# A two-layer generator backbone on one core: layer-1 modulation products taken out of layer 0, the others placed between token projections, half of the first output projection placed around the layer norm

## The reference, cut to what matters

```python
for i in range(DEPTH):                      # two layers
    mod_l = (c_act @ mod_w[i] + mod_b[i]).reshape(b, N_MOD, 1, d)
    mod_c = (c_ctx_act @ mod_w[i] + mod_b[i]).reshape(N_MOD, d)
    hl = modulate(rms_norm(xl, norm_g[i, 0]), mod_l[:, 0], mod_l[:, 1])
    if i % 2 == 0:
        yl = even_mixer(hl, *ew); yc = even_mixer(hc, *ew)
    else:
        ...                                 # latent attention and differential attention
    xl = xl + mod_l[:, 2] * yl
    h2l = modulate(rms_norm(xl, norm_g[i, 1]), mod_l[:, 3], mod_l[:, 4])
    xl = xl + mod_l[:, 5] * moe(h2l, ...)

def even_mixer(h, ...):
    u = h @ w_in                            # 1024 -> 1536
    y_conv = conformer_conv(u[..., :1024], ...)   # value * sigmoid(gate), 31 taps, layer norm, silu
    y_pool = pool_mix(u[..., 1024:], ...)         # windows 2, 4, 8, 16, then a 128 x 128 product per group
    return concatenate([y_conv, y_pool], -1) @ w_out
```

## Time and profile before

| | us |
|---|---|
| median of 3 runs | 1004.16 |
| lowest, highest | 1004.1, 1006.32 |
| the profiled execution | 1001.35 |
| its span | 999.6 |
| PE busy in the span | 861.9 (86%) |
| DVE, ACT, POOL busy | 322.8, 175.0, 184.0 |
| DMA traffic | 298.00 MB, mean 298 GB/s |

### The profile page before, as it was taken

The page is one execution under the profiler, slowest core; times in us unless marked ns, Lnnn a source line. Parts: engine busy times, 40 slices in busy tenths (PEclk is TensorE's granted clock), DMA queues, the critical chain, the costliest instruction groups (busy, mean ns, idle before and its releaser), DMA issues.

```text
span 999.6 us, 10053 instructions
## 1 busy us (share of the span) xinstructions
PE 861.9 (86%) x3779; PEld 384.6 (38%) x3779; DVE 322.8 (32%) x699; ACT 175.0 (18%) x465; POOL 184.0 (18%) x212
## 2 busy tenths in 40 slices
PE   1799989997999999887849999796696999978776
PEld 0444435444733333222228443354545433322222
DVE  1269996213511221110123331636305111111010
ACT  2400033212200000000032111535503000000000
POOL 3100690122112123201121220301111111111000
PEclk9899998998899999897969999999797899989998
DMA  9981289954799999999989105270247799999993
GB/s 366 408 324 71 84 365 424 429 212 168 264 359 403 338 397 406 392 405 419 422 347 372 54 24 229 91 330 1 81 172 251 275 404 408 412 420 426 414 421 135
DMA packets 33111, 298.00 MB, mean 298 GB/s; under 512 B 6464, under 2 KB 6770, under 8 KB 16156
## 3 DMA queue, kind: packets, MB, share of 16 engines
q1 hardware_dynamic: 26064, 283.26, 70.1%
q0 software_dynamic: 6912, 13.92, 4.0%
q10 hardware_dynamic: 76, 0.02, 0.0%
HBM read 293.66 MB, written 12.58 MB: 306 GB/s over the span
## 4 chain that ended last, share of the span: by engine, by line
PE 67%; DMA 18%; DVE 4%; ACT 3%; issue 3%; SPq 2%; POOL 1%; DVEq 0%; ACTq 0%; POOLq 0%
PE bank L1099 17%; PE bank L460 9%; DMA ring<-in_gu_pack 9%; PE bank L1001 8%; PE bank L1122 7%; PE bank L1192 6%; DMA ring<-in_mod_pack 6%; PE bank L938 5%; DMA B<-in_gu_pack 4%; PE bank L1203 3%; SPq L890 2%; PE bank L1050 2%; PE bank L965 2%; PE bank L948 1%; PE bank L540 1%
## 5 line engine op out<-in xcount | busy, mean ns | idle before, releaser
L1099 PE MATMUL bank<-ring,hT 128*64 128x512 f32 x704 | 208.1, 624 | 27.0 <-issue 18.2
L1803 DVE SCALAR_TENSOR_TENSOR hT<-hT,WORK,bank 128x256 f32<-128x256 f32 x34 | 16.3, 480 | 324.9 <-ACT hT L1360 312.2
L1099 PEld LDWEIGHTS bank<-ring,hT 128*64 128x64 f32 x704 | 61.8, 143 | 128.3 <-issue 126.4
L1887 DVE SCALAR_TENSOR_TENSOR WORK<-WORK,par 128x512 f32<-128x512 f32 x116 | 90.7, 860 | 0.0
L460 PE MATMUL bank<-ring,hT 128*128 128x512 f32 (+2 forms) x256 | 88.0, 499 | 0.7 <-ACT hT L1333 0.7
L1001 PE MATMUL bank<-ring,B 128*128 128x512 f32 x192 | 83.3, 594 | 0.0
L1122 PE MATMUL bank<-ring,WORK 128*64 128x512 f32 x352 | 79.9, 595 | 1.0 <-ACT WORK L1365 1.0
L1365 ACT ACTIVATE WORK<-bank 128x256 f32<-128x256 f32 x34 | 13.1, 384 | 279.3 <-PE bank L1108 279.3
L938 PE MATMUL bank<-ring,cs 128*32 128x512 f32 x384 | 48.7, 653 | 14.6 <-DMA ring<-in_mod_pack 14.6
L1192 PE MATMUL bank<-hT,ring 128*128 128x512 f32 x128 | 57.4, 612 | 2.9 <-ACT hT L1414 2.9
L460 PEld LDWEIGHTS bank<-ring,hT 128*128 128x128 f32 x256 | 46.0, 190 | 35.9 <-issue 34.0
(11 more groups left out here) (270 smaller groups left out, 1041.0 us busy)
## 6 DMA issues: line engine op xcount, KB each, us to landing
ring<-in_gu_pack SPq DMA_DIRECT2D x42, 2048.0 KB, 21.5
ring<-in_mod_pack SPq DMA_DIRECT2D x24, 2048.0 KB, 18.7
ring<-in_down_pack SPq DMA_DIRECT2D x21, 2048.0 KB, 29.6
WORK<-in_gu_pack SPq DMA_DIRECT2D x6, 2048.0 KB, 28.8
ring<-in_wout_pack SPq DMA_DIRECT2D x4, 2048.0 KB, 18.7
ring<-in_win_pack SPq DMA_DIRECT2D x3, 2048.0 KB, 36.8
X<-in_gu_pack SPq DMA_DIRECT2D x3, 2048.0 KB
B<-in_gu_pack SPq DMA_DIRECT2D x3, 2048.0 KB
```

What stands on the lines that cost most here:

```text
L1099: mm = pe.matmul(dst[ST * x:ST * x + ST, :], HG[L][s][:, k, :], columns(units[x], 512 * k, 512), start=k == 0, stop=k == KC - 1)
L1887: ins = dve.scalar_tensor_tensor(out=acc, in0=src, scalar=w, in1=acc, op0=ALU.mult, op1=ALU.add)
```

## The change

Only two pairs of layer-1 weights are moved to stand behind the first MoE (with the one that stood there already), and two more behind the layer-1 projection weights. Mods 2 to 5 are placed between the groups of value, gate and pool products, each turn one group behind its product. The products with the pooled half of the output projection's depth are made ahead of the convolution's transposes (tiles 0 and 1) and behind them (tile 2). One layer-1 mod (6) stays in layer 0, 7 stands behind the MoE, 8 and 9 among the projections, 10 and 11 in eight parts in the differential attention. The columns of mods 0, 1, 6 to 11 are written by DVE in one instruction. The order of the squares in layer 1 is split around the copy of mod 7.

```diff
@@ stream_plan
-    out += pair(1, 0) + [("wout", 0, 0)] + pair(1, 1) + [("wout", 0, 1)] + pair(1, 2)
+    out += [("wout", 0, 0)] + pair(1, 0) + [("wout", 0, 1)]
     out += expert_units(0)
-    out += pair(1, 3)
+    out += pair(1, 1)
     for kind in OIN:
         out.append(("oin", kind))
     out.append(("lora",))
-    out += pair(1, 4) + pair(1, 5)
+    for v in (2, 3, 4, 5):
+        out += pair(1, v)
@@ generator_kernel, banks
+        MOD_BANK = (6, 6, 6, 6, 6, 6, 7, 6, 6, 6, 7, 7)
-        OUT_BANKS = ((4, 5), (0, 1))
+        OUT_BANKS = ((4, 5, 6), (0, 1))
@@ project_pe
                 if i == MOD_ITEM:
-                    mod_multiply(10)
+                    mod_multiply(8)
+                elif i == MOD_ITEM + 4:
+                    mod_turn(8)
                 elif i == len(ITEMS):
-                    mod_multiply(11)
+                    mod_multiply(9)
@@ attention_pe
                     turn_o(i - 3)
+                if i == 2:
+                    mod_turn(9)
+                if 8 <= i < 16:
+                    mod_in_attention(i - 8)
                 if 0 <= i - 1 < n_units:
                     probs(i - 1)
@@ attention_scalar
+                if i == 12:
+                    mod_copy(10)
...
+            mod_copy(11)
@@ tensor: new functions
+            def mod_in_attention(j):
+
+                i, part = 10 + j // 4, j % 4
+                if part == 0:
+                    for h in (0, 1):
+                        loaded(pe, where[("mod",) + MOD_PAIRS[i] + (h,)])
+                    pe.wait_ge(sem("mod_cols"), 10)
+                    pe.wait_ge(sem("mod_rows"), i)
+                mm = mod_part(i, MOD_BANK[i], (2 * part, 2 * part + 1))
+                if part == 3:
+                    mm.then_inc(sem("mod_mm"), 1)
@@ tensor: layer 0
-            for i in range(2, 6):
-                mod(i)
+            for m in (0, 1):
+                value_gate(m, 1)
+                value_gate(m, 0)
+            mod_multiply(2)
+            value_gate(2, 1)
+            mod_turn(2)
+            mod_multiply(3)
+            value_gate(2, 0)
+            mod_turn(3)
+            value_gate(3, 1)
+            value_gate(3, 0)
+            pool_rows(0)
+            mod_multiply(4)
+            pool_rows(1)
+            pool_rows(2)
+            mod_turn(4)
+            pool_rows(3)
+            mod_multiply(5)
+            mod_turn(5)
 
             pe.wait_ge(sem("pool_w_in"), 16)
+            pe.wait_ge(sem("pool_in"), 4)
             pe.wait_ge(sem("pooled"), 4)
...
-            mod(6)
+            def out_half(i, ks):
+
+                h, j = divmod(i, NT)
+                w = slot(where[("wout", 0, h)])
+                loaded(pe, where[("wout", 0, h)])
+                for k in ks:
+                    mm = pe.matmul(bank[OUT_BANKS[0][i % 3]][:, :], mixT[:, (k + 4) % KC, j * P:(j + 1) * P], w[:, (k + 4) % KC, :], start=k == 0, stop=k == KC - 1)
+                return mm
+            pe.wait_ge(sem("mod_cols"), 6)
+            gates("a0", 0, 2, (0, 1), (6, 7))
+            pe.wait_ge(sem("pool_out"), 4)
+            out_half(0, range(4))
+            out_half(1, range(4))
             pe.wait_ge(sem("conv_done"), 4)
...
+            out_half(2, range(4))
+            mod_multiply(6)
+            pe.wait_ge(sem("ln_rows"), 4)
...
+            mod_turn(6)
+            for i in range(8):
+                if i >= 3:
+                    pe.wait_ge(sem("out_used"), i - 2)
+                    out_half(i, range(4))
+                for k in range(4, KC):
+                    if i == 0:
+                        pe.wait_ge(sem("mix_done"), k - 3)
+                    mm = out_half(i, (k,))
+                mm.then_inc(sem("out_mm"), 1)
...
-            mod(9)
+            mod(7)
@@ scalar: layer 1
-            mod_rows(9)
-            square_rows("a1")
+            square_rows("a1", (0, 1))
+            mod_copy(7)
+            square_rows("a1", (2, 3))
@@ vector: columns in one instruction, norm_rows
+            def mod_columns(i):
+
+                L, v = MOD_PAIRS[i]
+                r = R_MODB + 48 * L + 8 * v
+                dve.wait_ge(sem("mod_turned"), i + 1)
+                tt(mods[:, L, v, :, :].rearrange("p (h c) s -> p h c s", h=2), bank[7][:, 0:16].rearrange("p (c h s) -> p h c s", c=4, h=2),
...
                 if tag == "a1":
-                    for j in range(4):
+                    for j in (0, 1):
+                        scaled(tag, j)
+                    mod_columns(7)
+                    norm_scale(1, 0)
+                    for j in (2, 3):
                         scaled(tag, j)
```

More of the change, by code:

```diff
@@ L173, in slot_plan @@
             free = [at for at in free if at not in LENT]
+        if n > RING and all(stream[held[at]] in early or stream[held[at]][0] == "wout" for at in free if at in held) and len(free) == RING:
+            free.sort(key=lambda at: early.index(stream[held[at]]) if stream[held[at]] in early else len(early) + held[at])
         at = free.pop(0)
@@ L989, in moe_gates, with project_out @@
                     mm.then_inc(sem("gate_mms"), 1)
-            def project_out(L, lhs, tiles, first=0, between=None):
+            def project_out(L, lhs, tiles):
                 for h in range(2):
@@ L1178, in _, with value_gate @@
             mod(1)
-            for m in range(4):
+            def value_gate(m, part):
                 n = where[("win", m // 2)]
```

161 lines of the change are left out of this document (79 added, 82 removed).

## The result

| | before | after |
|---|---|---|
| median (4 runs each) | 1004.13 | 991.35 |
| lowest, highest | 1001.14, 1006.32 | 988.34, 994.82 |
| the profiled execution | 1001.35 | 988.34 |
| its span | 999.6 | 986.5 |

The ratio is 0.9888, 95% interval 0.9857 to 0.9919: the change gains 12.8 us of the median. The forecast, 1006, was wrong, and so was its sign; the time lies 0.15 us outside the range. Rival A, with 993.5, describes it.

A forecast was written before the change was run, and what follows sets the result against it. The way to the first expert product and the stretch between the MoEs bound the kernel. Terms +3.1 - 3.8 + 2.4 = +1.7 on the profiled 1001.35 gave 1003.0; the median's 2.8 above made it 1006, range 991.5 to 1009.5.

The forecast's parts named there:

- Rival A: Layer 0: POOL is served at once, `pooled` stays at 149.95; -10.7 in all, 993.5, chance 0.35.
- What bounds the kernel: The MoE moves as a block; the way to the first expert product and the stretch between the MoEs count.
- Step 1: Start of layer 0: eight small column operations become one on DVE, whose first block comes 0.8 us earlier.
- Step 2: Layer 0: POOL's third group starts 75.0 behind DVE's first block, after POOL was idle 1.0 us.
- Step 3a: Layer 0: POOL is shut out through DVE's last run; `pooled` at 162.4 instead of 149.95, layer 0's end +3.1.
- Step 4: Layer 0, from the pool products to the end of the output projection: 74.9 us.
- Step 5: Behind the first MoE: two squares ahead of mod 7's copy and columns on DVE bring -3.8 us.
- Step 6: Layer 1's projections and attention: turns and copies of the moved mods cost +2.4 us, quarters hidden.

The follow-up runs named there:

- e11_before_yield: The kernel before, with one break in DVE's run at tap 10 of the third block; 1003.66, ratio 1.0014.
- e1: The changed kernel, with POOL waiting for DVE's count of taps ahead of its groups three and four; 1002.78, ratio 0.999.
- e4: The changed kernel with no half of the output projection ahead of the layer norm; 992.15, ratio 0.9889.
- e6: The changed kernel with layer 1's squares not split, mod 7's copy ahead of all four; 995.09, ratio 0.9919.
- e7: The changed kernel with every quarter of mods 10 and 11 made twice, the second time with zeros; 995.08, ratio 0.9929.
- e9: The changed kernel with mod 7's columns on ACT again and the squares not split; 994.36, ratio 0.9914.
- e8: The kernel of e3 with one break in DVE's run, at tap 10 of the third block; 984.78, ratio 0.9831.
- e12: Mods 2 to 5 behind the pooled groups, DVE's break at tap 5, slots given out in the change's order; 992.03, ratio 0.9909.
- e10: The changed kernel in its own order, with one break in DVE's run at tap 23 of the third block; 987.83, ratio 0.9887.
- e5: The kernel of e2, with POOL's requests placed by waits on DVE's count of taps; one run, 1002.06.
- e2: The changed kernel with the first pooled groups ahead of the last block's value and gate products on PE; 991.64, ratio 0.9875.
- e3: The changed kernel with mods 2 to 5 behind all four pooled groups again, slots given out in that order; 988.82, ratio 0.985.

## Why the prediction was wrong

**What bounds the kernel: right.** The first MoE's steps took 211.7 before and 212.1 after; in the twelve runs they took 211.8 to 215.6, while they began up to 17 us apart. It moves as a block, with a scatter of its own.

**Step 1, start: too small.** -0.8 was forecast (bounds 0 and 1.1); PE's first group came 2.2 us earlier (42.27 and 40.03), DVE's first product 1.5. I had counted only mod 1's columns. Mod 0's had held up ACT's copies of the transposed rows (1 us) as well. In the other traces with the change's start DVE's first product comes at 55.3 to 56.9, and in e11_before_yield, with the old start, at 57.1. The means of old and new start (2 and 12 traces) differ by 1.5 us, and the scatter is as large.

**Step 2, when POOL gets its data: right.** 75.0 behind DVE's first product and an idle of 1.0 us were forecast; it was 75.4 and 0.72.

**Step 3a, POOL is shut out again: this failed.** The sentence was "By then DVE is back in an undisturbed run, the state in which 16.31 us were lost." I compared POOL's idle of 1.0 us with one multiply-add of 0.665 and took anything longer for a shut-out. But the one row of before that showed a shut-out stood behind six undisturbed multiply-adds and 72.58 us of idle POOL, and nothing told me what lies between one and six. The runs fill it in, with the undisturbed multiply-adds (one each 0.66 us) that DVE had begun when the request came:

| multiply-adds | POOL's instruction | where |
|---|---|---|
| 1 | 1.09 to 1.64 | after, e1, e4, e6, e7, e9, e8, e11, e12 |
| 2 | 1.09, 1.66, 1.66 | e11, e8, e10 |
| 3 | 1.12, 1.19 | e12 |
| 4 | 1.43, 1.54 | e5, e2 |
| 5 | 1.71 | e2 |
| 6, 0.25 us into the sixth | 1.44 | e1 |
| 6, 0.61 to 0.63 us into the sixth | 16.31, 16.31; 2.40, 2.41 with a break | before, e3; e8, e11 |
| 7, 8, 9 | 12.04, 10.72, 4.09: to the run's end | e5, e5, e1 |
| 20 | 7.09 to 7.10: to the run's end; 1.79 with a break | after, e1, e4, e6, e7, e9; e10 |

So the step is wrong by its threshold: `pooled` was complete at 149.72 and not at 162.4, and start and layer 0 together gave -9.6 us in place of +3.1. The latest request that was still served came 3.56 us into an undisturbed run, the earliest that was shut out 3.92 us into one (five times 0.6625 and the part of the sixth); this one came 0.25 us into it. Whether it is the time or the number of multiply-adds that counts stays open, since all are of one size. What a late `pooled` costs, nearly its whole length, e1_gap confirms; the 12 us themselves were in no run.

**Step 4: right.** 74.9 from the pool products to the end of the projection; measured 149.87 to 224.7, 74.8. Layer 0 came out 8.05 shorter, beside rival A's 8.5 (9.3 less the start).

**Step 5, behind the MoE: the size right by chance.** -3.8 was forecast, -3.1 is what the two profiles show. The 4.5 us from the request for x to its landing hold for its first half alone (the first square starts 4.5 to 5.4 us behind the request in the ten traces with the split); the second half comes at 8.0 to 9.4 (8.4 in the change) and holds the third square, so the split gains nothing (e6_nosplit). The gain is that of the columns, and it is there where mod 7's weights come late: 22.0 in the profile of before against 18.6 to 19.3 in the new order with a product as late. Where they come in time the old order takes 18.3 (e11), no more than the new one. So it is 0 to 3.4 us, by the execution. I had one execution, and took its wait of 6.35 us on a transfer for part of the kernel; in the fourteen traces this wait is 3.6 to 6.4.

**Step 6: too dear.** +2.4 was forecast, +1.3 is the difference of the profiles. In the traces this stretch has two levels, 2 us apart, which go with 65.2 or 67.1 in the stretch behind it: with the old layer 1 208.9 and 211.7 (before, e11), with the new 210.0 to 210.4 and 212.3 to 212.6 (e7_double left out). So it is near 1; where the two levels come from stays open. The quarters are hidden, as said, but the cover left is what remains of PE's own wait of 1.70, 0.5, not the 1.5 that I read from scores to maxima (e7_double).

**The sum.** Rival A said -10.7; the profiles show -13.1, the medians -12.8. Of the 2.4 between profiles and rival, 1.6 lie in the second MoE and 0.8 ahead of the first, in stretches that scatter by 3.5 us (201.4 to 204.9) and 7 us (50.5 to 57.4) over the fourteen traces; whether the change has a part in them stays open.

By the Trainium skill, "SBUF — State Buffer", SBUF: two separate sides, whichever of the two instructions starts first has the shared ports for that whole instruction and the other is blocked; its result was rival A. For requests up to 3.6 us into DVE's undisturbed run the runs agree (1.1 to 1.7 us); for later ones they don't (4.09, 7.09, 10.72, 12.04, 16.31).

## What to carry to other kernels

When two engines share something and one row shows a long wait, ask what state that row was in and how far the case at hand is from it. Between one row that shows a wait behind six multiply-adds and a case with one, nothing was known, and the rows nearest the case, in which the two engines took turns, deserved more than a third of the chance. Price each part of a large diff by the slack of the engine it serves: here the reordering, most of the lines, was worth nothing, the halves 2.3 us of layer 0 and the work taken away, by elimination, most of the rest. A single wait of DVE gained 4 us in one order and nothing in two others. A transfer's wait in a single profile is a draw, not a property of the kernel.

## What the runs showed of the hardware

- A run of DVE multiply-adds on two SBUF tensors starts one each 0.6625 us though each lasts 0.74 to 0.75: they overlap. A POOL instruction that reads SBUF and asks 3.56 us or less into an undisturbed run is served in 1.1 to 1.7 us; one that asks at 3.92 us or later waits to the end of the run, up to 16.31 us here.
- Ending the overlap once costs DVE 0.12 us (e8_yield: the start of tap 10 comes 0.78 behind the one before instead of 0.66) and lets POOL in, whether it waits at that moment (e8, e10, e11) or asks 1.8 us later (e12). From then on the two alternate, with a DVE multiply-add each 1.5 to 1.7 us.
- Taking turns is not free: 29 multiply-adds take 19.30 us alone and 32.0 to 35.7 where POOL works beside most of them. Letting POOL in earlier moves that loss forward, it doesn't remove it: the convolution ended 101.9 us behind DVE's first product in the change and 102.8 in e8_yield.
- PE's granted clock stood at 0.50 at the start of the work behind a wait of 1.57 us (e3_behind), 3.73 us (e11) and 5.00 us (the change). The pool products then took 6.46 (e3_behind) and 6.34 us (the change) instead of 4.1, the transposes 3.67 instead of 1.80 (e11). The wait of 1.57 us so cost 2.4 us beyond its own length. The waits of 0.72 us ahead of each turn did not do it (1.00 in e8_yield).
